# Down projections of two MLPs as pairs of output tiles with seven quarter products

## The reference

```python
D_FF = 4 * D_MODEL
def squared_relu_mlp(h, w1, w2):
    return jnp.square(jax.nn.relu(h @ w1)) @ w2
```

## Time and profile before

| | |
|---|---|
| time of the three runs | 1767.77, 1768.43, 1765.96 us; median 1767.77 |
| span of the profiled execution | 1764.2 us |
| mean granted TensorE clock | 0.996 of full speed |
| TensorE, VectorE, ScalarE, GpSimd busy | 98%, 45%, 38%, 50% of the span |

### The profile page before, as it was taken

One profiled execution on the slowest core, in us unless ns is written; L12 is line 12 of the kernel. 1 busy time (PEld: TensorE's weight loads), 2 busy tenths in 40 slices (PEclk: granted clock), 3 DMA queues, 4 the chain that ended last, 5 costly groups with the idle time before them and its releaser, 6 DMA issues.

```text
span 1764.2 us, 22985 instructions
## 1 busy us (share of the span) xinstructions
PE 1737.4 (98%) x8243; PEld 1445.3 (82%) x8243; DVE 785.8 (45%) x1225; ACT 662.9 (38%) x1039; POOL 876.9 (50%) x473
## 2 busy tenths in 40 slices
PE   8999999999999999999999999999999999999999
PEld 6887888888888877878888888889878888888887
DVE  6558654301331479956430133137856344444200
ACT  6338543312322456554321232135357332222221
POOL 3457545444444469755544444445445544444442
PEclk9999999999999999999999999999999999999999
DMA  5531123223333213123333332322210233332332
GB/s 190 133 98 59 37 72 107 95 95 96 96 96 99 80 48 108 60 84 95 103 99 96 96 95 95 95 84 72 87 49 14 95 95 96 97 101 98 96 107 71
DMA packets 46073, 158.45 MB, mean 90 GB/s; under 512 B 5744, under 2 KB 6000, under 8 KB 46000
## 3 DMA queue, kind: packets, MB, share of 16 engines
q1 hardware_dynamic: 46000, 157.45, 28.5%
HBM read 153.10 MB, written 2.10 MB: 88 GB/s over the span
## 4 chain that ended last, share of the span: by engine, by line
PE 90%; DVE 5%; ACT 2%; issue 1%; POOL 1%; DMA 0%; SPq 0%; DVEq 0%; POOLq 0%; ACTq 0%
PE PS L1834 26%; PE PS L1835 26%; PE PS L1836 26%; PE PS L1903 2%; DVE PS L1219 1%; PE PS L1939 1%; PE PS L1934 1%; PE PS L1935 1%; PE PS L2095 1%; PE PS L1844 1%; PE PS L1876 0%; PE PS L1976 0%; DVE PS L1211 0%; PE PS L2118 0%; PE PS L2119 0%
## 5 line engine op out<-in xcount | busy, mean ns | idle before, releaser
L548 POOL TENSOR_TENSOR wl<-raw,wh 128x1024 fp32r<-128x1024 f32 x216 | 523.0, 2422 | 623.2 <-ACT wh L742 198.3
L1835 PE MATMUL PS<-XLR,wh 128*128 128x512 f32 x1216 | 474.2, 390 | 0.0
L1834 PE MATMUL PS<-XHR,wh 128*128 128x512 f32 x888 | 348.8, 393 | 6.3 <-POOL wl L618 5.8
L1836 PE MATMUL PS<-XHR,wl 128*128 128x512 f32 x888 | 346.4, 390 | 0.0
L1834 PE MATMUL PS<-HH,wh 128*128 128x512 f32 x688 | 267.6, 389 | 0.0
L1835 PE MATMUL PS<-HL,wh 128*128 128x512 f32 x688 | 267.6, 389 | 0.0
L1836 PE MATMUL PS<-HH,wl 128*128 128x512 f32 x688 | 267.6, 389 | 0.0
L1835 PEld LDWEIGHTS PS<-XLR,wh 128*128 128x128 f32 x1216 | 229.1, 188 | 47.0
L728 ACT ACTIVATE wh<-raw 128x1024 fp32r<-128x1024 f32 x123 | 128.9, 1056 | 242.2 <-PE PS L1836 197.6
L1834 PEld LDWEIGHTS PS<-XHR,wh 128*128 128x128 f32 x888 | 167.4, 188 | 42.0 <-POOL wl L618 6.2
L1836 PEld LDWEIGHTS PS<-XHR,wl 128*128 128x128 f32 x888 | 167.4, 188 | 35.4
(11 more groups left out here) (344 smaller groups left out, 2561.6 us busy)
## 6 DMA issues: line engine op xcount, KB each, us to landing
raw<-weights SPq DMA_DIRECT2D x287, 512.0 KB, 3.5
X<-x_t SPq DMA_DIRECT2D x8, 256.0 KB, 6.7
out_t<-X SPq DMA_DIRECT2D x8, 256.0 KB, 4.7
KH<-rope_h SPq DMA_DIRECT2D x4, 128.0 KB, 4.7
KL<-rope_l SPq DMA_DIRECT2D x4, 128.0 KB, 5.5
QH<-XHR SPq DMA_DIRECT2D x16, 32.0 KB, 2.0
QL<-XLR SPq DMA_DIRECT2D x16, 32.0 KB, 2.0
pos_i<-positions SPq DMA_DIRECT2D x1, 256.0 KB, 8.5
```

The lines of the kernel that those rows point to most:

```text
L548: pool.tensor_tensor(wl[:, j], raw[:, j], wh[:, j].bitcast(F32), ALU.subtract).then_inc(w_lo, 1)
L1834: pe.matmul(out, wa, xa, start=start, stop=False)
L1835: pe.matmul(out, wa, xb, start=False, stop=False)
L1836: return pe.matmul(out, wb, xa, start=False, stop=stop)
```

## The change

A chunk now has 8 ff tiles, so there are four. Its down work goes by pairs of output tiles and pairs of ff tiles. A pair is a 2 × 2 block matrix, and so are the hidden values (two ff tiles × two halves of the 512 columns). Instead of eight quarter products it takes seven (A11, S1, A12, S2, S4, A22, S3): three use weight quarters as they are, four use sums of them, and the hidden side has four sums (T1 to T4) to match. Each product is 4 ff pairs × 3 matmuls of 256 columns. The last chunk does three pairs that way, its tile m = 6 whole before them and m = 7 whole behind them.

- VectorE makes the weight sums (`quad_sum`, into the PSUM areas SUM_A and SUM_B; S1 from two inputs in SBUF), their lows (`quad_low`), the hidden sums (`t_sums`, which the listings call `sqb`), five additions of products into `M` a pair (`read`), whose quarters hold a changed basis until `restore`, an instruction with two inputs in SBUF, puts it right in the last chunk.
- ScalarE makes the highs of the seven weight operands (`quad_high`) and of the hidden sums, and the squares of the outputs from `M`.
- GpSimd makes the lows of the three plain quarters (`quad_lows`) and of the hidden sums (`sums_low`), and adds the squares between them (`add_output`).
- On TensorE a lead up tile of the next chunk stands ahead of the pairs, and the first product waits for all hidden sums of its chunk.

The hunks are of the constants, GpSimd, ScalarE, VectorE and TensorE, in this order.

```diff
@@ -52,8 +52,15 @@
-CHUNK = 16
+CHUNK = 8
+HALF_S = S // 2
+QUADS = 4
+PRODUCTS = 7
+READS = 5
+LAST_PRODUCT = (0, 1, 4, 5, 6)
+H_RING = 5
+HID_PARTS = 2 * NCHUNK * CHUNK
...
@@ -587,6 +672,71 @@
+            def quad_lows(n0, u, which=(A11, A12, A22)):
+                q, n = QUAD0[n0] + u, n0 + 2 * u
+                for i, block, half in ((A11, n, 0), (A12, n, 1), (A22, n + 1, 1)):
+                    if i not in which:
+                        continue
+                    pool.wait_ge(quad_hi, PRODUCTS * q + i + 1)
+                    if i == A22:
+                        pool.wait_ge(quad_sums, 4 * q + 4)
+                    low = pool.tensor_tensor(quad_weight(wl, n0, u, i), raw_half(block, half),
+                                             quad_weight(wh, n0, u, i).bitcast(F32), ALU.subtract)
+                    if i == A22:
+                        low.then_inc(w_lo, 2)
+                    else:
+                        low.then_inc(side_lo, 1)
+            def sums_low(layer, p):
+                done = 2 * (4 * NCHUNK * layer + p)
+                for i, half in ((H_T1, 0), (H_T4, 1)):
+                    pool.wait_ge(sums_hi, done + half + 1)
+                    pool.tensor_tensor(parts(TL, p, i, 2), t_sums[:, S * half:S * half + S],
+                                       parts(TH, p, i, 2).bitcast(F32), ALU.subtract).then_inc(sums_lo, 1)
+            def mlp_lows(layer, job, after):
+                for c in range(NCHUNK):
+                    n0, _, quads = down_block(layer, c)
+                    for t in range(1 if c else 0, CHUNK):
+                        n = up_block(layer, c, t)[0]
+                        if n >= n0 - RING:
+                            quad_lows(n0, 0, ((A11,), (A12,), (A22,), ())[n - n0 + RING])
+                        else:
+                            lo_range(n + RING, n + RING + 1)
+                        if t % 2:
+                            sums_low(layer, 4 * c + t // 2)
+                        if c == NCHUNK - 1 and t == 2:
+                            pool.wait_ge(last_m_hi, layer + 1)
+                            pool.tensor_tensor(parts(TL, LAST_M, H11, 2), M[:, KT - 1],
+                                               parts(TH, LAST_M, H11, 2).bitcast(F32), ALU.subtract).then_inc(last_m_lo, 1)
+                    if c < NCHUNK - 1:
+                        for u in range(1, quads):
+                            quad_lows(n0, u)
+                        lo_range(n0 + 2 * quads, n0 + 2 * quads + RING)
+                add_output(job, 0)
...
@@ -977,39 +1129,109 @@
+            def quad_high(n0, h):
+                u, i = divmod(h, PRODUCTS)
+                q, n = QUAD0[n0] + u, n0 + 2 * u
+                if h < 8:
+                    sc.wait_ge(blocks_done, n0 - RING + h // 2 + 1)
+                else:
+                    sc.wait_ge(products_made, PRODUCTS * QUAD0[n0] + h - 8 + 1)
+                if i in (A11, A12, A22):
+                    block, half = {A11: (n, 0), A12: (n, 1), A22: (n + 1, 1)}[i]
+                    sc.wait_ge(raw_in[block % RING], 16 * (block // RING + 1))
+                    x = raw_half(block, half)
+                else:
+                    sc.wait_ge(quad_sums, 4 * q + {S1: 2, S2: 3, S4: 3, S3: 4}[i])
+                    x = SUM_A if i in (S1, S4) else SUM_B
+                sc.activation(quad_weight(wh, n0, u, i), x, ACT.Copy).then_inc(quad_hi, 1)
+            def mlp(layer, entry, job):
...
+                    p = 4 * c + t // 2
+                    sc.wait_ge(sums_made, 4 * NCHUNK * layer + p + 1)
+                    sc.activation(parts(TH, p, H21, 2), squared(1), ACT.Copy).then_inc(hid_hi, 1)
+                    for i, half in ((H_T1, 0), (H_T4, 1)):
+                        sc.activation(parts(TH, p, i, 2), t_sums[:, S * half:S * half + S], ACT.Copy).then_inc(sums_hi, 1)
...
@@ -1500,41 +1723,155 @@
+            def quad_sum(n0, u, i):
+                q, n = QUAD0[n0] + u, n0 + 2 * u
+                if i == S1:
+                    v.wait_ge(raw_in[(n + 1) % RING], 16 * ((n + 1) // RING + 1))
+                    tt(SUM_A, raw_half(n + 1, 0), raw_half(n + 1, 1), ALU.add).then_inc(quad_sums, 1)
+                elif i == S2:
+                    v.wait_ge(raw_in[n % RING], 16 * (n // RING + 1))
+                    v.wait_ge(quad_sums, 4 * q + 1)
+                    tt(SUM_B, SUM_A, raw_half(n, 0), ALU.subtract).then_inc(quad_sums, 1)
+                elif i == S4:
+                    v.wait_ge(quad_sums, 4 * q + 2)
+                    tt(SUM_A, SUM_B, raw_half(n, 1), ALU.subtract).then_inc(quad_sums, 1)
+                else:
...
+                def odd_sums(c, t):
+                    t1, t3, t4, t2 = [t_sums[:, i * HALF_S:(i + 1) * HALF_S] for i in range(4)]
+                    tt(t3, odd[:, right], even_kept[:, right], ALU.subtract)
+                    step(tt(t2, odd[:, right], t1, ALU.subtract))
+                    sig(tt(t4, t2, odd[:, left], ALU.subtract), sums_made, 4 * NCHUNK * layer + 4 * c + t // 2 + 1)
...
+                def read(c, u, j):
+                    n0, T0, _ = down_block(layer, c)
+                    r = READS * (QUAD0[n0] + u) + j
+                    v.wait_ge(products_made, PRODUCTS * (QUAD0[n0] + u) + LAST_PRODUCT[j] + 1)
+                    v.wait_ge(products_read, r)
...
+                def restore(u, done):
+                    v.wait_ge(products_read, done)
+                    d = quarters(u)
+                    tt(d[:, 1:3], d[:, 3:4].broadcast_to((P, 2, HALF_S)), d[:, 1:3], ALU.subtract).then_inc(restored, 1)
...
+                    for t in range(1 if c else 0, CHUNK):
+                        hidden(c, t)
+                        if t == 6:
+                            quad_low(n0, 0, S1)
+                            quad_sum(n0, 0, S4)
+                        if t % 2 == 0:
+                            even_low(c, t)
                         else:
-                            v.tensor_copy(M[:, m], PS[:, T % 4]).then_inc(bank_free, 2)
-                            v.wait_ge(bank_free, T + 2)
-                last_output(out_job, T0 + KT - 1)
+                            odd_sums(c, t)
+                            if t == CHUNK - 1:
+                                quad_low(n0, 0, S2)
+                                quad_sum(n0, 0, S3)
+                            odd_low(c, t)
+                        if t == 4:
+                            quad_sum(n0, 0, S1)
+                            quad_sum(n0, 0, S2)
+                        if last and t == 1:
+                            restore(KT // 2 - 1, READS * QUAD0[n0])
+                    if last:
+                        v.wait_ge(blocks_done, n0)
+                        sig(tt(M[:, KT - 2], M[:, KT - 2], PS[:, (T0 - 1) % 4], ALU.add), bank_free, T0)
+                        quad_low(n0, 0, S4)
+                    else:
+                        hidden(c + 1, 0)
+                        quad_low(n0, 0, S4)
+                        even_low(c + 1, 0)
+                    for u in range(quads):
+                        more = u + 1 < quads
+                        if more:
+                            quad_sum(n0, u + 1, S1)
+                        quad_low(n0, u, S3)
+                        read(c, u, 0)
+                        if more:
+                            quad_sum(n0, u + 1, S2)
+                        read(c, u, 1)
+                        if last and u:
+                            restore(u - 1, READS * (QUAD0[n0] + u))
+                        if more:
+                            quad_low(n0, u + 1, S1)
+                            quad_sum(n0, u + 1, S4)
+                            quad_low(n0, u + 1, S2)
+                        read(c, u, 2)
+                        if more:
+                            quad_sum(n0, u + 1, S3)
+                        read(c, u, 3)
+                        if more:
+                            quad_low(n0, u + 1, S4)
+                        read(c, u, 4)
+                    if last:
...
@@ -2153,35 +2491,98 @@
-                        open_tile(T0 + m)
-                        last = m == KT - 1
-                        out = PS[:, RB if last else (T0 + m) % 4]
-                        for b in range(2):
-                            open_block(n0 + 2 * m + b)
-                            if m == 0:
-                                pe.wait_ge(hid, h0 + SLOTS * (b + 1))
-                            for k in range(SLOTS):
-                                x = SLOTS * b + k
-                                ins = products(out, *weight(n0 + 2 * m + b, k), HH[:, x], HL[:, x],
-                                               x == 0 and (c == 0 or not last),
-                                               x == CHUNK - 1 and (c == NCHUNK - 1 or not last))
-                            ins.then_inc(blocks_done, 1)
...
+                def product(c, u, i, out, operand):
+                    n0 = down_block(layer, c)[0]
+                    q = QUAD0[n0] + u
```

(112 more changed lines are left out.)

301 lines of the change are left out of this document (202 added, 99 removed).

## The result

The changed kernel takes 1806.72 us (median of 4 runs, 1804.96 to 1810.23) against 1767.18 for the kernel before: ratio 1.0228, 95% interval 1.0213 to 1.0242. That is 39.5 us more, above the range of the prediction and on the side to which it gave 0.39. The span of the profiled execution is 1804.7 us, 40.5 above that of before, and the mean granted clock 0.983.

What follows compares the result with a forecast made beforehand. TensorE, busy 98% of the span, was taken as the bound: 28.2 us saved less 24.0 of gaps and 3.2 at layer ends gives 1.0 less, a 1763.2 us span and a 1767 us median, range 1755 to 1790.

Steps and rivals of the forecast that it cites:

- the side to which it gave 0.39: Whole kernel: chance of a slower time, against 0.37 for faster and 0.24 for the same.
- What bounds the kernel, and that time comes back as waits of TensorE: Whole kernel: TensorE busy 98% of the span; only less TensorE work saves time, and making it wait costs time.
- 256 columns at 0.118: Downs: a 256-column matmul takes 0.118 us, saving 14.1 us a layer, 28.2 for both.
- The long train of 264 columns: Trace of another loop: 0.1203 us a matmul, used as one end for the 256-column price.
- the 148.5: Downs after the change: time in us estimated by the skill's issue-gap formula, against 165.7 before; 34 saved for both layers.
- Left are 3.0 us, eight times: Chunk ends: first product waits for hidden sums until 8.45 us, lead tile covers 5.44; 24.0 us lost in all.
- The clock as a rival at 0.16: Rival, gaps at chunk ends: clock falls after idling, 2.4 us lost each, eight cost 19: 1786 us; chance 0.16.
- Pairs paced by TensorE, S1's sum hidden: Pairs: VectorE 9.5 us against TensorE's 9.9; S1's sum loses about 0.8 to GpSimd's low, costed at nothing.
- The rival that VectorE becomes the bound: Rival, pairs: VectorE takes 11.3 us against TensorE's 9.9, 32 us in all, near 1799; chance 0.07.
- the 0.8 that I had put on each: Pairs: us lost by each S1 sum, with two SBUF inputs, on meeting GpSimd's A11 half-block low.
- A wait costs every product a start: Rival, pairs: 210 products' semaphore waits at 0.11 us each cost 23 us: 1790 us; chance 0.07.
- The end of a layer, 1.6: Last pair and m = 7: restore, squares and additions delay GpSimd's lows; two waits of 0.8 us, 3.2 for both layers.

Runs made afterwards that it cites:

- the versions further ahead: Changed kernel with wait moved to S1 and S2, sums' lows first, first chunk reordered, VectorE another tile ahead there; variants measured 1765.70, 1761.69, 1761.15 and 1761.93 us.
- the joined version: Changed kernel with wait moved to S1 and S2, sums' lows first, first chunk reordered, ScalarE's high of tile 6 earlier: 1764.30 us, 0.9980 of the kernel before.
- the run further ahead: The joined version with VectorE one tile further ahead in the first chunk, order of S2's low, S3's sum and odd low unaltered: 1761.69 us, 0.9961.
- the next one: The run further ahead, plus the lead tile's low and sum moved from ahead of the pairs to the last pair: 1761.15 us, 0.9955.

## Why the prediction was wrong

- *What bounds the kernel, and that time comes back as waits of TensorE:* right. The measured loss lies in waits and their after-effects, and the pairs have no holes of note at full clock.
- *256 columns at 0.118:* mis-sized: measured 0.1195 in 316 matmuls, 3.8 us less saved than forecast. The long train of 264 columns was the better guide. The figure of the Trainium skill that the prediction named beside it (109 ns, "TensorE: Matmul & The Clock Gate", section "Back-to-back issue gap") is still further off. Two slips in the working change nothing: the 148.5 worked out from that figure comes to 148.3, and the multiplications of all the downs fall by 11.7%, since two tiles stay whole.
- *"Left are 3.0 us, eight times":* the chain was right for the six later gaps, 3.13 and 3.12 (0.80 and 2.35 in the last chunks), and the run with GpSimd's lows first showed its last link (1.59 us with A22's low out of the way, 1.9 expected). It failed in the first chunk, by 16.5 us, the largest miss: the chain starts "on the last up tile after 0.20", which takes VectorE to be waiting for TensorE. That is so in the middle of a layer, where the earlier trace rows was read, and not at its start. The earlier trace rows had the sign of it: TensorE waiting for a bank that VectorE had not freed, at 273.28. The price of catching up, 8.0 us for two tiles in place of 6.1, and the halved number of tiles to do it in, were not worked out.
- *The clock as a rival at 0.16:* the sum put it at nothing, and this is the second step that failed, by 12.9 us. Neither step alone explains the time: by the account, with the clock's part gone the MLPs would be 26 us longer than before, and with the first chunk's gone 22. With both gone it is 10, a time of 1777, inside the range. I took from one stretch that the clock falls after 3.4 to 3.9 us of idle time, and that gaps of 3.0 end before that. The gaps end before it, and the clock falls all the same with TensorE at work again, up to 0.7 us later in the changed kernel and up to 1.6 in the versions further ahead. In the joined version it fell behind one gap of 3.02 us and not behind one of 3.03; of two gaps of 2.32 in the run further ahead both cost it, of two of 2.3 in the next one only the first. Behind the gaps of 1.59 and 1.70 it did not fall in the profiled executions, but it did behind the two waits of 1.63 ahead of the sum of squares. What decides it is not shown. The price, 1.5 us, is less than the 2.4 of the rival.
- *Pairs paced by TensorE, S1's sum hidden:* right. The rival that VectorE becomes the bound is out: with the clock up, 304 matmuls took 36.30 us. S1's sum does meet GpSimd's lows, and so does S3's, which takes both inputs from SBUF too and which the prediction left out. The 60 such sums took 0.78 us on the mean in the changed kernel, and one of 1.42 in the joined version began in a GpSimd low. That agrees with the rule of the Trainium skill ("SBUF — State Buffer", section "Who interferes with whom"). The one of 1.42 began 0.41 us into that low and cost 0.7 more than the 0.69 alone, near the 0.8 that I had put on each; but in the changed kernel only 22 of the 60 overlap a weight low of GpSimd's, so the mean is 0.09 more.
- *A wait costs every product a start:* out. The pitch over 316 matmuls includes 26 such waits.
- *The end of a layer, 1.6:* 1.09 ahead of m = 7 (forecast 0.8), and nothing behind it. Not forecast: 0.93 us in the first chunk, for a weight low behind lows of sums, and the 0.80 and 0.47 ahead of m = 6.

## What to carry to other kernels

A chain of lags read in the middle of a loop holds where the engines stand to each other as they do there; at the first pass ask who is behind whom, and whether there are passes enough to catch up. Count a gap in TensorE's work at its length and the half clock that can follow it, even where the gap is shorter than the one that a trace happened to show. And before a wait is covered with work, look which of the instructions behind it needs what is waited for: a moved wait and four orders of instructions turned 2.3% of loss into 0.4% of gain, with the same arithmetic.

## What the runs showed of the hardware

- The granted clock can fall after the idle time is over: at 1.00 through 3.13 us of standing still, at 0.58 in the 4.1 us of full work that followed.
- Equal gaps are not equally dear: 3.02 us cost 1.5 us in one layer and 3.03 us cost nothing in the other, in the same execution.
- 256-column matmuls came every 0.1195 us at full clock, against 0.1134 for half of a 512-column one: for halves of this size 5% is lost.
